# One decoder layer in float32: gates computed first and kept in DRAM, branch products split in three, one block instead of two

## The reference, cut to what matters

```python
gates = jax.nn.sigmoid((h @ w_gate[l] + b_gate[l]).astype(jnp.float32))
gates = gates.astype(x.dtype).reshape(b, s, N_BRANCH, D_MODEL)
merged = (gates[:, :, 0] * (o_a @ w_o_a[l])
          + gates[:, :, 1] * (o_b @ w_o_b[l])
          + gates[:, :, 2] * (o_m @ w_o_m[l]))
x = x + merged @ w_out[l]
x = x + conv_ffn(rmsnorm(x, ffn_norm[l]), w_up[l], conv_w[l], conv_b[l], w_down[l])
```

## Time and profile before

| | us |
|---|---|
| median of 3 runs | 1987.96 |
| the runs | 1984.94, 1987.96, 2330.19 |
| span of the profiled execution, first to last instruction | 1979.5 |
| PE busy in it | 1859.2 (94%) |
| DVE, POOL, ACT busy | 710.4, 581.4, 539.1 |

### The profile page before, as it was taken

One profiled execution on the slowest core, in us unless ns is written; L12 is line 12 of the kernel. 1 busy time (PEld: TensorE's weight loads), 2 busy tenths in 40 slices (PEclk: granted clock), 3 DMA queues, 4 the chain that ended last, 5 costly groups with the idle time before them and its releaser, 6 DMA issues. The chain is left out here.

```text
span 1979.5 us, 23310 instructions
## 1 busy us (share of the span) xinstructions
PE 1859.2 (94%) x8777; PEld 1483.2 (75%) x8777; DVE 710.4 (36%) x1318; ACT 539.1 (27%) x1029; POOL 581.4 (29%) x503
## 2 busy tenths in 40 slices
PE   4799999998877979999999989899999999999999
PEld 3577999986665856666666668688888888888887
DVE  4634223235666431111111153242444243424343
ACT  4434223233344431111111142322122212221221
POOL 5445235343232211111111053242133213321321
PEclk8899999998999989999999999899999999999999
DMA  5202002000010042111110060221122102210102
GB/s 197 83 32 65 1 1 64 1 17 14 2 42 1 1 88 54 45 38 35 38 45 24 0 198 1 64 85 32 32 64 64 41 23 64 64 42 21 43 22 85
DMA packets 112818, 90.75 MB, mean 46 GB/s; under 512 B 16812, under 2 KB 97388, under 8 KB 112748
## 3 DMA queue, kind: packets, MB, share of 16 engines
q1 hardware_dynamic: 112748, 89.81, 15.1%
HBM read 85.54 MB, written 4.26 MB: 45 GB/s over the span
## 5 line engine op out<-in xcount | busy, mean ns | idle before, releaser
L1779 PE MATMUL ps<-act_hi,f_hi 128*128 128x512 f32 x704 | 274.7, 390 | 6.3 <-DVE f_lo L1547 6.3
L1779 PE MATMUL ps<-act_lo,f_hi 128*128 128x512 f32 x704 | 274.6, 390 | 0.0
L1779 PE MATMUL ps<-act_hi,f_lo 128*128 128x512 f32 x704 | 274.5, 390 | 0.0
L1547 POOL TENSOR_TENSOR f_lo<-merged,f_hi 128x1024 fp32r<-128x1024 f32 x65 | 156.6, 2438 | 83.7 <-ACT f_hi L1628 83.7
L1320 PE MATMUL ps<-act_hi,g_hi 128*128 128x512 f32 x384 | 170.5, 444 | 3.2 <-DVE g_lo L1303 3.2
L1027 PE MATMUL ps<-w_hi,act_hi 128*128 128x512 f32 x320 | 160.4, 501 | 8.1 <-DVE attn_out L709 4.8
L1779 PEld LDWEIGHTS ps<-act_hi,f_hi 128*128 128x128 f32 x704 | 132.7, 188 | 34.1 <-DVE f_lo L1547 6.6
L1292 DVE TENSOR_TENSOR gate<-ps,gate 128x512 f32<-128x512 f32 x48 | 33.2, 692 | 345.4 <-PE ps L1330 345.4
L1330 PE MATMUL ps<-attn_out,o_w 128*128 128x512 f32 x320 | 148.3, 602 | 6.8 <-ACT o_w L1244 3.2
L1734 DVE TENSOR_TENSOR attn_out<-ps,attn_out 128x512 f32<-128x512 f32 x160 | 106.1, 686 | 134.6 <-PE ps L1799 134.6
L1779 PEld LDWEIGHTS ps<-act_hi,f_lo 128*128 128x128 f32 x704 | 132.6, 188 | 27.6
(11 more groups left out here) (198 smaller groups left out, 3340.0 us busy)
## 6 DMA issues: line engine op xcount, KB each, us to landing
merged<-in_w_up_dram SPq DMA_DIRECT2D x44, 512.0 KB, 4.0
g_raw<-in_w_gate_dram SPq DMA_DIRECT2D x23, 512.0 KB, 3.9
merged<-in_w_down_dram SPq DMA_DIRECT2D x22, 512.0 KB, 3.5
attn_out<-in_x_dram SPq DMA_DIRECT2D x16, 512.0 KB, 5.0
attn_out<-in_w_in_dram SPq DMA_DIRECT2D x20, 384.0 KB, 4.0
w_raw<-in_w_in_dram SPq DMA_DIRECT2D x12, 384.0 KB, 3.3
w_raw<-in_w_out_dram SPq DMA_DIRECT2D x16, 256.0 KB, 3.7
out_dram<-attn_out SPq DMA_DIRECT2D x8, 512.0 KB, 2.6
```

The source lines that it names most:

```text
L1547: eng.tensor_tensor(f_lo[:, b, :], f_raw[b], f_hi[:, b, :].bitcast(F32), ALU.subtract).then_inc(f_lo_done[b], 1)
L1779: ins = pe.matmul(ps[:, 2 * q + half, :], w[:, q, k * P:(k + 1) * P], a[:, k, half * 512:(half + 1) * 512], start=(k == 0 and i == 0), sto ...
```

## The change

`gated_outputs` and `output_projection` become one function and one block, `gates_and_outputs`, without a barrier between them. In it:

- The 24 gate sums (8 feature tiles x 3 branches, two halves each) come first. After each, ACT writes the sigmoid into one of three full-width buffers, and SP stores it to a DRAM tensor `gates` (512 KB each, 24 of them).
- Meanwhile ACT and DVE split the mixers' result into `attn_hi` and `attn_lo` (10 tiles of 128x1024).
- The branch products come second, as three split products: 20 x 3 matmuls for each feature tile in place of 20 plain ones. SP loads three gates back for each feature tile, and the branch weights are split (`o_hi` by ACT, `o_lo` by POOL) through one staging buffer. DVE multiplies and adds as before, with one add less for each half (no copy for the first branch).
- A feature tile of `merged` is split as soon as it is done, by ACT and POOL, while PE is at the next. Pieces of `w_out` are loaded after the last branch weights are split, and the output projection follows in the same streams.
- All loops of the stage are written out; `w_out` pieces have places of their own in a region that reuses the branch operands' memory (`WO_SLOT`, `wo_free`).

The core of the diff:

```diff
+        gates_dram = nc.dram_tensor("gates", (NK * 3, P, S), F32, kind="Internal").ap()
...
+O_TILES = [(0, 2), (2, 4), (6, 4)]
+WO_SLOT = [1, 2, 7, 8, 9, 10, 3, 4, 5, 6, 11, 12, 13, 14, 15, 0]
...
+        def wo_free(eng, n):
+            eng.wait_ge(out_summed, UN * (NK - 1) + (2 if n < 2 else 4 if n < 6 else UN))
+            if n >= 10:
+                eng.wait_ge(added, 4 * NK)
...
+            def load_o_weights(f):
+                cols = slice(f * P, (f + 1) * P)
+                if f == 0:
+                    sp.wait_ge(g_lo_first, 1)
+                else:
+                    sp.wait_ge(o_lo_done, BR * f)
...
+            def store_gate(n):
+                sp.wait_ge(gate_done, 2 * n + 2)
+                sp.dma_start(gates_dram[n], gate[:, n % BR, :]).then_inc(gate_out[n % BR], 16)
+
+            def load_gate(n):
+                f, b = n // BR, n % BR
+                sp.wait_ge(gate_out[b], 16 * NK)
+                if f >= 1:
+                    if b == 0:
+                        sp.wait_ge(weighed, UN * (f - 1) + 2)
+                    else:
+                        sp.wait_ge(added, 4 * (f - 1) + 2 * b)
+                sp.dma_start(gate[:, b, :], gates_dram[n]).then_inc(gate_in[b], 16)
...
+            for n in range(BR):
+                load_gate(n)
+            load_o_weights(1)
+            for f in range(1, NK):
+                for b in range(BR):
+                    load_gate(BR * f + b)
+                if f + 1 < NK:
+                    load_o_weights(f + 1)
+            sp.wait_ge(o_lo_done, BR * NK)
+            for n in range(NS):
+                if n >= NRAW_O:
+                    sp.wait_ge(wo_lo_done, n - NRAW_O + 1)
                 load_w_out(sp, w_out, wo_raw, wo_in, n)
+                if 6 <= n < 6 + NT:
+                    t = n - 6
+                    sp.wait_ge(out_summed, UN * NK)
                     sp.dma_start(x1[:, t, :], x_t[t]).then_inc(res_in[t // 2], 16)
...
+            def cast_o_weights(f, b):
+                i0, tiles = O_TILES[b]
+                act.wait_ge(o_in, 64 * (f + 1))
+                if f >= 1:
+                    act.wait_ge(out_summed, UN * (f - 1) + 2 * b + 2)
+                act.activation(o_hi[:, i0:i0 + tiles, :], o_raw[:, i0:i0 + tiles, :], ACT.Copy).then_inc(o_hi_done, 1)
...
+            for f in range(NK):
+                if f >= 1:
+                    low_merged(f - 1)
+                if f + 1 < NK:
+                    for b in range(BR):
+                        low_o_weights(f + 1, b)
+            for n in range(6):
+                low_w_out(n)
+            low_merged(NK - 1)
+            for n in range(6, NS):
+                low_w_out(n)
...
+            for n in range(NG):
+                wait_g_low(pe, n)
+                for half in range(2):
+                    u = 2 * n + half
+                    if u >= 4:
+                        pe.wait_ge(gate_done, u - 3)
+                    for k in range(NK):
+                        for i, (w, a) in enumerate(((g_hi, act_hi), (g_hi, act_lo), (g_lo, act_hi))):
...
+            pe.wait_ge(attn_lo_done, AT)
+            for f in range(NK):
+                for b in range(BR):
+                    pe.wait_ge(o_lo_done, BR * f + b + 1)
...
+                        if at >= 4:
+                            pe.wait_ge(weighed, at - 3)
+                        for i in range(tiles):
+                            for m, (w, a) in enumerate(((o_hi, attn_hi), (o_hi, attn_lo), (o_lo, attn_hi))):
```

More of the change, by code:

```diff
@@ L1197, in gated_outputs @@
[L1197 to L1203, removed]
+        gain, sums, rstd = x1_stats[:, 0:NK], x1_stats[:, NK:NK + NT], x1_stats[:, NK + NT:NK + 2 * NT]
@@ L1207, in _, with load_gate_weights @@
         def _(sp):
[L1208 to L1219, removed]
+            def load_gate_weights(n):
+                f, b = n // BR, n % BR
+                if n >= 3:
+                    sp.wait_ge(g_lo_done, n - 2)
+                sp.dma_start(g_raw[:, n % 2], w_gate[0].rearrange("(k p) n -> p k n", p=P)[:, :, (b * NK + f) * P:(b * NK + f + 1) * P]
+                             ).then_inc(g_in[n % 2], 16)
+            def load_o_weights(f):
[4 more added lines that the diff above has]
+                    sp.wait_ge(o_lo_done, BR * f)
                 sp.dma_start(o_raw[:, 0:2], w_o_a[0].rearrange("(k p) n -> p k n", p=P)[:, :, cols]).then_inc(o_in, 16)
@@ new lines, in _ @@
+            with nc.allow_non_contiguous_dma(reason="one bias or gain per partition"):
+                sp.dma_start(bias[:, 0:BR * NK], b_gate[0].rearrange("(k p) -> p k", p=P)).then_inc(vectors_in, 16)
+                sp.dma_start(gain, ffn_norm[0].rearrange("(k p) -> p k", p=P)).then_inc(vectors_in, 16)
+            load_gate_weights(1)
+            load_gate_weights(2)
+            for n in range(NG):
+                if n + 3 < NG:
+                    load_gate_weights(n + 3)
+                if n == 2:
+                    load_o_weights(0)
+                store_gate(n)
@@ L1439, in _, with weigh @@
         def _(dve):
+            dve.wait_ge(g_hi_done, 1)
+            dve.tensor_tensor(g_lo[:, 0], first_gate, g_hi[:, 0].bitcast(F32), ALU.subtract).then_inc(g_lo_first, 1)
+            for i in range(AT):
+                dve.wait_ge(attn_hi_done, i + 1)
+                dve.tensor_tensor(attn_lo[:, i, :], attn_out[:, i, :], attn_hi[:, i, :].bitcast(F32), ALU.subtract
+                                  ).then_inc(attn_lo_done, 1)
+            def weigh(f, b, half):
+                at = UN * f + 2 * b + half
+                if half == 0:
+                    dve.wait_ge(gate_in[b], 16 * (f + 1))
+                dve.wait_ge(out_summed, at + 1)
+                dst = merged[:, f, HALF[half]] if b == 0 else gate[:, b, HALF[half]]
+                dve.tensor_tensor(dst, ps[:, 4 + at % 4, :], gate[:, b, HALF[half]], ALU.mult).then_inc(weighed, 1)
@@ new lines, in add @@
+            def add(f, b, half):
+                dve.wait_ge(weighed, UN * f + 2 * b + half + 1)
+                if b == 2:
+                    dve.wait_ge(added, 4 * f + half + 1)
+                dst = merged[:, f, HALF[half]]
+                dve.tensor_tensor(dst, dst, gate[:, b, HALF[half]], ALU.add).then_inc(added, 1)
+            for f in range(NK):
+                for b in range(BR):
+                    for half in range(2):
+                        weigh(f, b, half)
+                        if b >= 1 and half == 1:
+                            add(f, b, 0)
+                            add(f, b, 1)
@@ L1446, in _ @@
-            for k in range(NK):
-                dve.wait_ge(m_hi, k + 1)
-                dve.tensor_tensor(act_lo[:, k, :], merged[:, k, :], act_hi[:, k, :].bitcast(F32), ALU.subtract).then_inc(m_lo, 1)
-            dve.wait_ge(gain_in, 16)
+                                  gain.unsqueeze(2).to_broadcast([P, NK, P]), ALU.mult).then_inc(x1_gained, 1)
+            dve.wait_ge(vectors_in, 32)
             for n, (t, half) in enumerate(SUMS):
@@ L1480, in share @@
                 t, half = SUMS[n]
[L1481 to L1482 removed]
+                slot = WO_SLOT[half * NK + k]
+                for i, (a, w) in enumerate(((act_hi, 0), (act_hi, 1), (act_lo, 0))):
+                    ins = pe.matmul(ps[:, n % 4, :], a[:, k, t * P:(t + 1) * P], wo[:, slot, w, :],
                                     start=(k == 0 and i == 0), stop=(k == NK - 1 and i == 2))
```

337 lines of the change are left out of this document (156 added, 181 removed).

## The result

Times are medians. Every ratio is the recorded one, to runs of the kernel before that belong to the same series, since the kernel before took from 1980 to 1990 us over all series. The run of 2330.19 us is a slow execution, with a lower granted clock, and enters no ratio.

The account below looks back on a forecast made before the run. PE, busy 1859.2 of 1979.5 us, was taken as the bound. 49.8 + 2.9 - 0.7 - 1.5 = 50.5 us gained gives a span of 1929.0; with 8.5 from span to median, 1937.5 us, range 1931 to 1954.

Parts of the forecast that it names:

- The first term: First gate matmul to output projection: 422.2 us falls to 372.4 with 1632 split matmuls at 0.2267 us, gaining 49.8 us.
- 0.4 at each of six returns to a gate sum: Steady feature tile, old order: PE loses 0.4 us at each of six returns from branch products to gate sums.
- the border and the late `o_w`: 6.0 us at the old blocks' border, 5.42 of them idle, and the first tile's 3.2 us wait for o_w go.
- The start: First gate matmuls run at half clock: 12 steps take 5.1 us instead of 2.7, so 2.4 us stay charged.
- All feed-forward and input work stays as it is: Feed-forward and input parts: no change in time, nothing charged.
- The two supply terms: Late first branch-weight reload where the gates turn round, 0.7 us lost (0 to 3); late w_out pieces, 1.5 lost.
- The restart: Output projection start: without the idle gap PE stays at 2.4 GHz, gaining 2.9 us over 14 steps.
- all three supply terms: Branch weights through one staging buffer, the gates' turnaround, w_out pieces: upper bounds 4, 3, 5 us against charged 0, 0.7, 1.5.
- Late branch weights in each tile, 2: Product stage: branch-weight chain 2 us late for seven tiles, 14 us, total 1951; chance 0.16.
- Late `w_out`, 3: Output projection: w_out late by 5 us at its second half, 2 or 3 at first pieces, total 1943; chance 0.12.
- Borders that cost a drain, 4: Product stage: each of 48 borders between short sums costs 0.3 us, total 1952; chance 0.05.
- The clock, 5: Product stage: short stops drop PE to 1.2 GHz, up to 96 us for 480 matmuls, total 2033; chance 0.05.

Follow-up runs that it names:

- a_nospill: Changed kernel without the 24 stores and 24 reloads of the gates: 1940.99 us, ratio 0.9776 to the kernel before.
- a_best: Changed kernel with half_power moved ahead of act_hi and 128 unused bytes added, so all PE operands start at 192 modulo 256: 1927.73 us, ratio 0.9724.
- a_twice: Changed kernel with a 512 KB DRAM-to-DRAM copy behind each of the 24 gate loads: 1947.02 us, ratio 0.9811 to the kernel before.
- b_three_nodrain: Kernel before with three-pass branch products (unsplit stand-in operands) and without PE's wait for its own gate sum: 1943.91 us, ratio 0.9791.
- a_join: Changed kernel with one PE wait added, so the output projection begins only when all of merged is split: 1952.88 us, ratio 0.9825.
- a_plain: Changed kernel with each branch product as one plain float32 matmul in the new order: 1965.16 us, ratio 0.9913 to the kernel before.
- b_nodrain: Kernel before without PE's wait for its own gate sum after each second half: 1972.83 us, ratio 0.9953.

## Why the prediction was right, and where it was not

**The first term (49.8, measured 45.9).** Its mechanism held piece by piece. Three passes for a plain product: 29.2, the prices said 29. No wait for the own sum: 0.38 each, it said 0.3. Together (29.2 + 9.2) / 8 = 4.8 a tile, it said 4.9. One attribution fell: the "0.4 at each of six returns to a gate sum" is no cost of returning, since plain products in a row cost the whole 0.856. And the border and the late `o_w` went. What failed in this term is the price: 0.2267 us for each of 1632 split matmuls, taken from the old placement. 1152 at 0.2289 and 480 at 0.2311 make 374.6 in place of 370.0. The start cost 1.7 and not 2.4; it varies between executions, 2.4 again in `a_nospill`. With the old price restored, `a_best` takes 1097.21 - 725.53 = 371.7, against the forecast's 372.4.

**"All feed-forward and input work stays as it is"** was the costliest sentence. The same instructions on moved operands took 6.3 us more. In the output projection the new distance costs 384 x 6 ns = 2.3.

**The two supply terms (-0.7 and -1.5) did not occur.** PE waits for no branch weight and no piece of `w_out`; the latter's old lateness of 0.8 is gone too. The margin at the first reload is 1.0 us where the prediction had 0.6 for the turn of the gates, and `a_twice` shows that it is a real edge.

**The restart (2.9)** held in kind: after has no slow step there, and `b_three_nodrain`, with the same 5.42 us idle as before, runs its first 8 steps in 3.54 us at the low clock. Its size differs between executions: 1.7 us in that kernel and 1.7 in `a_join` after 7.6 us idle, where the trace of before had 2.9.

**The sum.** 1929.0 + 4.6 + 2.3 + 6.3 for the dearer matmuls, - 0.7 for the start, - 2.2 - 0.8 for what was not late, - 1.5 since the input part ended earlier in this execution: 1937.0, against 1936.7. With equal starts the span is 1927.9, 1.1 under the forecast. That the median forecast of 1937.5 came within 2.4 us of 1939.86 is in large part luck: 13 us of dearer matmuls were not foreseen, and the 8.5 us that were added to get from span to median are 3.2 for after, since most of the 8.5 was one quick execution of before.

One bound was added up wrong. With the upper bounds of all three supply terms (4, 3 and 5) the forecast becomes 1937.5 + 12 - 2.2 = 1947, not 1945. Nothing hung on it, since no supply term occurred.

**The rivals.** Late branch weights in each tile, 2: no such wait. Late `w_out`, 3: none. Borders that cost a drain, 4: product-stage sums of 6 and 12 matmuls in `a_best` go on at 226.7 ns across 48 borders. The clock, 5: 1.00 in the window of the product stage, with a bank change every 6 or 12 matmuls. The Trainium skill's rule on cycling through PSUM banks (TensorE: Matmul & The Clock Gate, section A second HAM failure mode: psum-queue depth-cycling) did not show in it.

## What to carry to other kernels

When a change adds or drops an SBUF tensor, compare the start bytes of the operands of all later matmuls, and read the distance between matmul starts in the code that was not changed. Price each edit of a reordering by itself in the old order: here two small edits gave 38.4 of the 45.9 us, on PE, with the splitting left out. A profiled span is compared with a span; the distance to the median is not a constant of the kernel.

## What the runs showed of the hardware

- The start of stationary and moving operand, modulo 256 bytes, sets the distance of 128x512 split matmuls: equal 226.7 to 227.8 ns, unequal 228.9 to 233.4, in seven kernels. With unequal starts the same stage, at the same placement, ran at 228.9 in `after` and at 233.4 in `a_join`, and the up projection of `after` changed from 233.4 to 229 on its way. Why is open. The alternating steps of 512 and 256 columns in the input projections showed no gain from equal starts; no stage of another width alone was tried.
- A plain float32 matmul of 128x512 takes 0.856 us in a row, 3.78 split ones (`a_plain`).
- PE's wait for its own last sum costs 0.38 us each time, at full clock (`b_nodrain`).
- After 5.4 us of idle time PE ran 8 to 14 steps at the low clock (1.7 to 2.9 us lost: `b_three_nodrain`, before), after 2.57 us none (`a_twice`).
- 24 stores and 24 loads of 512 KB beside dense PE work cost PE nothing, at a mean of up to 165 GB/s (`after`, `a_nospill`).
